# A two-layer decoder step on one core: opening in parts, layers written out, waits by chunk, last square straight to TensorE

## What is computed

```python
x = x + 0.5 * swiglu(rms(x))                  # FFN 1: 1024 -> 2816 -> 1024
h = rms(x); z = h @ w_in                      # 5120 columns: q, k, v of four groups, two gates
A, B = dilated_attention(z), window_attention(z)   # against caches of up to 2048 rows
x = x + (sigmoid(ga) * (A @ w_branch_a) + sigmoid(gb) * (B @ w_branch_b)) @ w_out
x = x + 0.5 * swiglu(rms(x))                  # FFN 2
# after both layers
y = x * rsqrt(mean(x * x) + eps) * gain
```

## Time and profile before

| | us |
|---|---|
| median of three runs | 1549.99 |
| the profiled execution | 1550.88 |
| its span (first to last instruction) | 1549.1 |
| TensorE busy with matmuls | 1501.6 (97% of the span) |
| VectorE, ScalarE, GpSimd busy | 822.8, 681.4, 361.6 |

### The profile page before, as it was taken

How to read it: one execution, slowest core, us unless ns; L and a number is a source line. 1 busy time by engine, 2 the same in 40 slices (tenths; PEclk the granted TensorE clock), 3 DMA queues, 4 the chain that set the end, 5 groups by cost and what they waited for, 6 DMA issues and landing times.

```text
span 1549.1 us, 33560 instructions
## 1 busy us (share of the span) xinstructions
PE 1501.6 (97%) x11346; PEld 1426.1 (92%) x11346; DVE 822.8 (53%) x1327; ACT 681.4 (44%) x1179; POOL 361.6 (23%) x359
## 2 busy tenths in 40 slices
PE   7999999999999999999999999999999989999996
PEld 6999999988768899999999999999877689999996
DVE  6555446855334655554455554477544257555445
ACT  5444444554433444444444444455544335444443
POOL 4222212211103332221122221132111052322210
PEclk9999999999999999999999999999999999999998
DMA  8885566667684688646678846666776746984564
GB/s 327 313 295 179 166 202 210 227 223 247 233 276 147 225 291 298 210 132 203 213 294 291 281 142 193 206 221 205 241 251 236 250 140 238 327 298 152 155 203 149
DMA packets 95290, 352.11 MB, mean 227 GB/s; under 512 B 12368, under 2 KB 23888, under 8 KB 92496
## 3 DMA queue, kind: packets, MB, share of 16 engines
q1 hardware_dynamic: 95184, 350.77, 68.1%
HBM read 345.61 MB, written 94.37 MB: 284 GB/s over the span
## 4 chain that ended last, share of the span: by engine, by line
PE 86%; issue 6%; DMA 3%; POOL 3%; DVE 1%; ACT 1%; POOLq 0%; SPq 0%; DVEq 0%; ACTq 0%
PE ps L638 26%; PE ps L640 25%; PE ps L639 25%; DMA kvc<-in_kcache 2%; PE ps L849 2%; PE ps L863 2%; POOL ma L1460 1%; DMA kvc<-in_vcache 1%; PE ps L722 1%; PE ps L790 1%; PE ps L757 1%; PE ps L714 1%; POOL ssq L1410 1%; POOL mlo L1463 0%; PE ps L780 0%
## 5 line engine op out<-in xcount | busy, mean ns | idle before, releaser
L1159 DVE TENSOR_TENSOR wlo<-raw,whi 128x1024 fp32r<-128x1024 f32 (+2 forms) x420 | 492.3, 1173 | 497.0 <-ACT whi L972 496.6
L638 PE MATMUL ps<-xhi,whi 128*128 128x320 f32 x2048 | 647.0, 316 | 13.4 <-DVE wlo L1159 12.2
L640 PE MATMUL ps<-xhi,wlo 128*128 128x320 f32 x2048 | 634.9, 310 | 0.0
L639 PE MATMUL ps<-xlo,whi 128*128 128x320 f32 x2048 | 634.7, 310 | 0.0
L972 ACT ACTIVATE whi<-raw 128x1024 fp32r<-128x1024 f32 (+2 forms) x420 | 404.2, 964 | 313.8 <-PE ps L640 313.6
L638 PEld LDWEIGHTS ps<-xhi,whi 128*128 128x128 f32 x2048 | 385.9, 188 | 34.9 <-issue 28.7
L639 PEld LDWEIGHTS ps<-xlo,whi 128*128 128x128 f32 x2048 | 386.6, 189 | 0.5
L640 PEld LDWEIGHTS ps<-xhi,wlo 128*128 128x128 f32 x2048 | 386.4, 189 | 0.0
L640 PE MATMUL ps<-act_hi,wlo 128*128 128x320 f32 x704 | 217.6, 309 | 0.0
L639 PE MATMUL ps<-act_lo,whi 128*128 128x320 f32 x704 | 217.6, 309 | 0.0
L638 PE MATMUL ps<-act_hi,whi 128*128 128x320 f32 x704 | 217.6, 309 | 0.0
(11 more groups left out here) (122 smaller groups left out, 1287.7 us busy)
## 6 DMA issues: line engine op xcount, KB each, us to landing
out_new_a_sample<-in_cache_a SPq DMA_DIRECT2D x128, 510.0 KB, 5.8
raw<-in_ffn_gate SPq DMA_DIRECT2D x90, 512.0 KB, 4.0
raw<-in_ffn_up SPq DMA_DIRECT2D x90, 512.0 KB, 5.2
raw<-in_w_in SPq DMA_DIRECT2D x80, 512.0 KB, 4.2
kvc<-in_kcache SPq DMA_DIRECT2D x52, 512.0 KB, 5.3
kvc<-in_vcache SPq DMA_DIRECT2D x52, 512.0 KB, 4.5
raw<-in_ffn_down SPq DMA_DIRECT2D x64, 384.0 KB, 3.2
raw<-in_ffn_down SPq DMA_DIRECT2D x64, 320.0 KB, 3.0
```

Of the source, the lines that this page charges most:

```text
L638: pe.matmul(out, w0, hi, start=first, stop=False)
L639: pe.matmul(out, w0, lo, start=False, stop=False)
L640: return pe.matmul(out, w1, hi, start=False, stop=last)
L1159: nc.vector.tensor_tensor(wlo[:, (base + s) % RING, 0:tiles * P], raw[:, (base + s) % RAW, 0:tiles * P], whi[:, (base + s) % RING, 0:tiles ...
```

## The change

1. The gains are loaded from ScalarE's queue; `x` parts and the halves of units 0 and 1 alternate on SyncE's queue. ScalarE and VectorE take two chunks of `x` and one half unit in turn. The squares of the opening are two wide ScalarE instructions, added by three VectorE ones, in place of eight and eight.
2. TensorE first does 20 matmuls of ones (128 columns, float32), then `start_units`: runs over units 0 and 1 by half units and pairs of chunks. `sum_squares` stands behind unit 2.
3. The loop over the two layers is written out on every engine; the inner loops stay. The loads and splits of units behind the last layer go.
4. w_out: TensorE waits chunk by chunk, six chunks for output 0, six for output 1, then chunks 6 and 7 for both.
5. End: the squares of chunks 0 to 6 go to TensorE as their sum, that of chunk 7 goes in as a second matmul into the same bank, past GpSimd. ScalarE writes `x * gain` beforehand and has its table for the root loaded early; VectorE multiplies by `rinv` in four instructions of 640 columns.

```diff
-LOADS = (("x", 0), ("w", 0), ("x", 1), ("x", 2), ("w", 1), ("x", 3), ("w", 2), ("w", 3))
+LOADS = (("x", 0), ("a", 0), ("x", 1), ("a", 1), ("x", 2), ("b", 0), ("x", 3), ("b", 1), ("w", 2), ("w", 3))
+START_RUNS = ((0, (0, 1)), (0, (2, 3)), (1, (0, 1, 2, 3)), (0, (4, 5)), (1, (4, 5)), (0, (6, 7)), (1, (6, 7)))
+WARM = 20
...
-            with sp.Fori(0, DEPTH) as L:
+            for L in range(DEPTH):
...
-                first_units(L, U_GU[f], L * 3 + 2 * f, first_gate_up)
-                gate_up(0, (2, 3))
+                if L == 0 and f == 0:
+                    start_units()
+                    gate_up(0, (2,))
+                    sum_squares(0)
+                    gate_up(0, (3,))
+                else:
+                    first_units(L, U_GU[f], L * 3 + 2 * f, first_gate_up)
+                    gate_up(0, (2, 3))
...
-                        pe.wait_ge(mlo_done, L * KD + KD - 1)
-                        w_out(0, range(KD - 1))
-                        pe.wait_ge(wlo_done, L * NU + U_WO + 1 + RAW + 1)
-                        w_out(1, range(KD - 1))
-                        pe.wait_ge(mlo_done, L * KD + KD)
                         for o in range(2):
-                            w_out(o, (KD - 1,)).then_inc(unit_used, 1)
+                            pe.wait_ge(wlo_done, L * NU + U_WO + o + RAW + 1)
+                            for k in range(W_OUT_AHEAD):
+                                pe.wait_ge(mlo_done, L * KD + k + 1)
+                                w_out(o, (k,))
+                        for k in range(W_OUT_AHEAD, KD):
+                            pe.wait_ge(mlo_done, L * KD + k + 1)
+                            for o in range(2):
+                                mm = w_out(o, (k,))
+                                if k == KD - 1:
+                                    mm.then_inc(unit_used, 1)
...
-            sum_squares(3 * DEPTH)
+            last = 3 * DEPTH
+            pe.wait_ge(ssq_done, last * (KD + 1) + KD)
+            pe.matmul(ps[:, BK_O, 0:TOK], ones[:, :], ssq[:, :], start=True, stop=False)
+            pe.wait_ge(sq_done, (last + 1) * KD)
+            pe.matmul(ps[:, BK_O, 0:TOK], ones[:, :], sq[:, (KD - 1) % 2, :], start=False, stop=True)\
+                .then_inc(ms_ready, 1)
```

More of the change, by code:

```diff
@@ L348, in build @@
         gains_in = sem("gains_in")
+        half_in = [sem(f"half_in{s}") for s in range(2)]
+        half_hi = sem("half_hi")
+        half_lo = sem("half_lo")
+        tree_done = sem("tree_done")
         const_in = sem("const_in")
@@ L662, in first_units, with start_units @@
                         .then_inc(unit_used, 1)
+            def start_units():
+                seen = 0
+                for run, (s, ks) in enumerate(START_RUNS):
+                    if ks[0] < KD // 2:
+                        pe.wait_ge(half_lo, s + 1)
+                    else:
+                        pe.wait_ge(wlo_done, RAW + s + 1)
+                    for k in ks:
+                        if k >= seen:
+                            pe.wait_ge(xs_ready, k + 1)
+                            seen = k + 1
+                        mm = product(ps[:, s, 0:TOK], s, k, xhi[:, k, :], xlo[:, k, :], k == 0, k == KD - 1)
+                    if ks[-1] == KD - 1:
+                        mm.then_inc(unit_used, 1)
             def ffn_products(L, f):
@@ L948, in mixer_products @@
                     if m == 0:
-                        pe.wait_ge(mlo_done, L * KD + KD - 1)
-                        w_out(0, range(KD - 1))
-                        pe.wait_ge(wlo_done, L * NU + U_WO + 1 + RAW + 1)
-                        w_out(1, range(KD - 1))
-                        pe.wait_ge(mlo_done, L * KD + KD)
-                        for o in range(2):
-                            w_out(o, (KD - 1,)).then_inc(unit_used, 1)
+                        for o in range(2):
+                            pe.wait_ge(wlo_done, L * NU + U_WO + o + RAW + 1)
[7 more added lines that the diff above has]
+                                if k == KD - 1:
+                                    mm.then_inc(unit_used, 1)
             pe.wait_ge(set_up, 2)
-            with pe.Fori(0, DEPTH) as L:
+            for _ in range(WARM):
+                pe.matmul(ps[:, BK_O, 0:P], ones[:, :], ones[:, :], start=True, stop=True)
+            for L in range(DEPTH):
                 ffn_products(L, 0)
@@ L1026, in ffn_act @@
                     down(i, "same")
-                down(KD // 2 - 1, "next")
+                down(KD // 2 - 1, "end" if L == DEPTH - 1 and f == 1 else "next")
             def mixer_act(L):
@@ L1138, in mixer_act, with start_half @@
                     round_x(L * 3 + 2, m, m % 2)
[L1140 to L1147 removed]
+            def start_half(s, b):
+                cols = slice(b * HALF_UNIT, (b + 1) * HALF_UNIT)
+                act.wait_ge((raw_in if b else half_in)[s], 16)
+                nc.scalar.activation(whi[:, s, cols], raw[:, s, cols], ACT.Copy).then_inc(whi_done if b else half_hi, 1)
+            act.dma_start(gains[:, :, :], a["gains"]).then_inc(gains_in, 16)
+            act.wait_ge(set_up, 2)
+            nc.scalar.activation(rms[:, 0:1], eps[:, :], ACT.Copy)
+            act.wait_ge(gains_in, 16)
+            for part in range(XPARTS):
+                act.wait_ge(x_in[part], 16)
+                for m in (2 * part, 2 * part + 1):
+                    nc.scalar.activation(xhi[:, m, :], x[:, m, :], ACT.Copy, scale=gain(0, m)).then_inc(xhi_done, 1)
+                start_half(part % 2, part // 2)
+            round_unit(0, 0, 0, 0, 2, UT)
+            for h in range(2):
+                m = slice(h * KD // 2, (h + 1) * KD // 2)
+                nc.scalar.activation(sq0[:, m, :], x[:, m, :], ACT.Square).then_inc(sq_done, KD // 2)
+            round_unit(0, 0, 0, 0, 3, UT)
+            for L in range(DEPTH):
                 ffn_act(L, 0)
@@ L1206, in down @@
                                 add_to_x(L, BK_DN + o, i * 2 + o, i * 2 + R_DN[f] + o, 0.5)
-                            rest_unit(L, U_DN[f] + 4, i, 8, 4 * o + s,
-                                      UT if o == 1 and tail == "next" else DN_TILES[s])
-                        rest_x(norm, i * 2 + o)
+                            if not (o == 1 and tail == "end"):
+                                rest_unit(L, U_DN[f] + 4, i, 8, 4 * o + s,
+                                          UT if o == 1 and tail == "next" else DN_TILES[s])
+                        if norm < 3 * DEPTH:
+                            rest_x(norm, i * 2 + o)
                 gate_up(0, True, (UT,) * 4)
@@ L1424, in ffn_pool @@
                 clear_squares(norm)
-                with pool.Fori(0, KD // 2) as i:
+                for i in range(KD // 2):
                     for o in range(2):
-                        add_squares(norm, i * 2 + o, o)
+                        if not (norm == 3 * DEPTH and i == KD // 2 - 1 and o == 1):
+                            add_squares(norm, i * 2 + o, o)
             def mixer_pool(L):
@@ L1467, in mixer_pool @@
                     add_squares(norm, m, m % 2)
-            clear_squares(0, True)
-            for m in range(KD):
-                add_squares(0, m, m % 2)
-            with pool.Fori(0, DEPTH) as L:
+            for L in range(DEPTH):
                 ffn_pool(L, 0)
```

80 lines of the change are left out of this document (50 added, 30 removed).

## The result

The changed kernel took 1534.57 us (median of four runs, 1533.01 to 1537.47); the kernel before, run beside it, 1553.04 us (1547.8 to 1557.02). The ratio is 0.9876, 95% interval 0.984 to 0.9913: 1.24% faster. The forecast was 1532, between 1527 and 1539. The profiled execution took 1533.01 us with a span of 1530.9 us, 18.2 us less than before, where the steps summed to 18.8. So the saving was right to 0.6 us, but only because two steps that were wrong nearly cancelled: the opening gave 2.4 us more than forecast, the mixers took 2.2 us. That they cancelled is luck.

What follows compares the result with a forecast made beforehand. TensorE, busy with matmuls in 97% of the span, was taken as the bound. Savings of 4.7 + 8.9 + 3.4 + 1.8 = 18.8 us from 1550.9 gave 1532.1, so 1532 us, range 1527 to 1539.

Steps and rivals of the forecast that it cites:

- Start of the second layer: TensorE's stop there is the branch back; writing the loop out removes stop and slow matmuls, 4.7 us.
- The rival at 1536.8: At the second layer's start TensorE really waits for VectorE's `wlo`, so the 4.7 us stay; chance 0.09.
- the one at 1574: Slower: inner FFN loops at new places pay a fetch each turn, a nine-turn gate-up loop giving 1574; chance 0.04.
- w_out: Before w_out, chunk-wise waits remove TensorE's stop and the slow matmuls behind it: 4.45 us in each layer, 8.9 us.
- End: After the last sum into x: earlier square, faster second matmul and four wider multiplications save 3.4 us.
- Opening: At the kernel's start: earlier products, but a 3.1 us stop before unit 4 and slow matmuls behind it; gain 1.8 us.
- The fixed chain from the sum to unit 4: In the opening: root, reciprocal, gate product, SiLU, rounding and split take 6.9 us, plus 0.2 until unit 4 starts.
- upper bound of 4.1: The opening's most favourable gain, 4.1 us: products start at 7.9 and the clock does not fall.
- Nothing: Dropped loads and splits, layer index as constants, and the mixer's cache waits change nothing: together -1 to +2 us.

Runs made afterwards that it cites:

- the loop alone: The kernel before with only its loop over the two layers written out on all five engines: 1550.01 us, ratio 0.9982.
- again: The changed kernel run once more with no edit: 1536.29 us, ratio 0.9887 to the kernel before.
- old w_out: The changed kernel with the waits of the kernel before at w_out (seven chunks, then the eighth): 1546.77 us, one run.
- by way of GpSimd: The changed kernel with GpSimd adding the eighth square at the end and one matmul over the whole sum: 1537.26 us, one run.
- table load free: The changed kernel with ScalarE's wait for the constants moved behind the root of the mixer's norm: 1535.07 us, ratio 0.9869.

## Why the prediction was right, and where it was not

*Start of the second layer* (4.7 us). Right, to the tenth: 4.7 in the whole change, 4.7 with the loop alone, and TensorE's own branch took 4.91 us in the kernel before, 2.1 of them under products. The releaser in the earlier trace rows (`wlo`) named an instruction that had nothing to do with the stop. The count behind it (unit 208 split at 768.7, no stop at the border from FFN to mixer) was the sound argument. The rule cited there from the Trainium skill ("Runtime: NRT & Kernel Launch", instruction fetch mechanics) agrees with this run: the taken branch took 4.91 us and the untaken one 0.08, and with no taken branch there is no stop. That the time goes into a fetch isn't in any row. The rival at 1536.8 is out. So is the one at 1574: the eight written-out copies of inner loops show no stop at their turns, and each branch back of the gate and up loops takes 0.21 us (0.24 at most).

*w_out* (8.9 us). Right: 4.3 and 4.1, 8.3 in all. The last `mlo` is late by 0.25 us, as computed. Of the missing 0.6 us, 0.1 in each layer lies behind w_out, where the next FFN starts 0.55 us after the last matmul in place of 0.45; 0.1 in each is the new w_out itself (10.14 and 10.13 us from its first branch matmul on, 10.04 by the forecast's steps), and 0.2 is that the old one was that much shorter in layer two. One thing the sum took for certain: in the kernel before the clock fell behind both stops. With the old waits in other kernels (the loop alone, the old waits before w_out) it fell behind the second only, and there they cost 2.8 and 4.2 us. The new w_out takes 10.66 to 10.69 us in every trace that has it.

*End* (3.4 us). Right, 3.15. The second matmul took 0.81 us where 0.70 was assumed, and the square started 0.63 us after the last sum into x, not 0.48 + 0.1. Four multiplications took 3.03 us where 3.3 was the estimate. Of the 3.15 us the path past GpSimd is 1.0 by its run. By the rows of the two ends, the rest is ScalarE's square, which no longer has an unused unit in front of it (1.38 us after the sum into x in the earlier trace rows, 0.63 now: 0.75), the matmuls of the sum, once 1.43 us behind a stop of 3.19 and now 0.81 (0.62; with GpSimd in the path again they took 0.81 as well, behind a stop of 2.19) and the wider multiplications (3.79 to 3.03: 0.76). Those three were not tried one by one.

*Opening* (1.8 us). The mechanism was right, the size wrong: 4.2 us. The fixed chain from the sum to unit 4 came out 0.3 us shorter than computed (6.82 us, forecast 6.9 + 0.2), the stop before unit 4 is there, released by `wlo`. Two terms were off in this execution. The ones ended at 7.3, not 8.6, which brought the sum to 18.59 instead of 19.2: only 0.6 us of the 1.3, since a half unit was not there when TensorE asked for it (a stop of 0.39 us at 12.32 for `wlo`), against the forecast. With the shorter chain unit 4 came at 25.4 instead of 26.3: 0.9 us. And after a stop of 2.1 us the clock stayed up: 1.6 us. This is the upper bound of 4.1, and a little more. In another execution of the same opening the ones end at 8.8 and unit 4 starts at 26.29 (the number forecast), and in some the clock falls: up to the last down product of the first FFN the gain against 247.84 is 4.2 us, 3.4 (again), 3.4 (old w_out), 2.6 (by way of GpSimd) and 2.0 (table load free). So the step's error was to put a certain value on something that varies by 2 us between executions; its middle, about 3, is still above 1.8.

*Nothing* (-1 to +2). This is the step that failed. It held that constants in place of registers change nothing but the loads that go. They changed which instruction carries a wait: the sum's semaphore moved onto the table load, and 1.28 us of loading came onto the path of each mixer's norm, 1.06 us of it at TensorE, in both layers, 2.1 us. It is shown by the loop alone (8.22 us from sum to `qk` there too) and by its removal (7.16). Net, the mixers lost 2.2 us in the profiled executions (-0.7 and +2.9), which looks like these 2.1 us but isn't: 1.7 us less of waits for cache tiles and a slow stretch of 1.4 us in mixer 2 nearly cancelled. "The mixer's waits for caches" were part of this step as well, put at nothing, and they vary by some 2 us in each mixer. The moved wait was to be seen beforehand in ScalarE's order of instructions with the waits named. A page's rule belongs beside it: the Trainium skill ("ScalarE: Activation LUTs", section on what the table load costs) gives some 1.3 us for the load and about as much again for a drain. The load agrees (1.28 us); the drain is not seen, since the root starts 0.02 us behind the load's end in the rows above.

Had the opening come at 1.8 us, the time would have been some 1535.4 (1533.0 + 2.4), within the range too: the total tests the sum, and hardly its parts.

*What stays open.* Whether the clock falls behind a stop of 1.8 to 3 us isn't decided by the stop's length in these traces: 1.77 us let it fall in the mixer of the changed kernel and 2.24 not in that of the kernel before, 2.10 and 2.61 us before unit 4 once and once not, and at w_out 3.06 did and 3.07 didn't. And the slow level at the start ended after 2.8, 3.9 and 5.7 us of products in the three runs without ones, but lasted until 18.92 in the old opening, whose products come in threes with holes of some 0.1 us between them and one stop of 1.03. In the trace of the loop alone, with the same old opening, it ended at 12.8 and came back from 16.55 on. That the holes prolong it is argued from these traces, not tried by itself.

## What to carry to other kernels

A loop that is written out takes the instructions on its register away, and with them the place where a wait was held: list the semaphores of each instruction before and after, above all where a table load stands in front of one. Where a stop's named releaser ended long before, count what the next instruction really needs, and look at the durations of the loop's branch: a taken one over a long body can be the stop, and the slow stretch behind it is part of its price. And where parts of a kernel vary by more than an edit is worth, measure the edit between two fixed points of the program, not by the total.

## What was not expected of the hardware

- A taken branch back over a layer took 4.91 us on TensorE, one over an inner loop 0.21 us, an untaken one 0.08 us.
- Matmuls of ones ahead of the first product were worth 0.1 us at unit 4 in the pair of single traces. Products themselves at the slow level (0.267 us from start to start) were followed by full speed after 2.8, 3.9 and 5.7 us in three executions.
- The 20 matmuls of ones (40 passes of 128 columns) took 5.8 us in one execution and 7.4 in another.
- In these kernels the mixer's root with two waits has one of them in front of its table load, and the load then does not start until it is met (root 2.08 us after the sum's start, 0.74 with one wait).
- The clock fell behind a wait of 1.77 us once and stayed up behind one of 3.07 us.
- A 512 KB load took 6.7 to 8.1 us in six traces with 1.2 MB of constants in the queue ahead of it, and 4.5 and 4.0 us in two without.
